# Turning query and index stacks with float32r products instead of pass-through turns

## The reference, cut to what matters

```python
iq = rope_partial(iq.reshape(bsz, t, IDX_HEADS, IDX_DIM), pos)      # 4 heads of 64
ik = rope_partial(ik, pos)
s = jnp.einsum('bthd,bsd->bths', iq, ik_all) * IDX_DIM ** -0.5
score = jnp.einsum('bth,bths->bts', iw, jax.nn.relu(s)) * IDX_HEADS ** -0.5
_, idx = lax.top_k(jnp.where(causal, score, -jnp.inf), topk)         # 256 keys a query
logits = jnp.einsum('btngd,btsnd->btngs', qg, kg) * HEAD_DIM ** -0.5 # 8 query, 2 key heads of 64
p = jax.nn.softmax(jnp.where(valid, logits, -jnp.inf), axis=-1)
o = jnp.einsum('btngs,btsnd->btngd', p, vg)
```

## Time and profile before

| | us |
|---|---|
| median of 3 runs | 1306.44 (1304.9 to 1308.1) |
| the profiled execution's own time | 1305.35 |
| its span | 1303.6 |
| PE busy | 1263.4 (97%) |
| DVE / POOL / ACT busy | 857.0 / 733.3 / 670.5 |

### The profile page before, as it was taken

The page is one execution under the profiler, slowest core; times in us unless marked ns, Lnnn a source line. Parts: engine busy times, 40 slices in busy tenths (PEclk is TensorE's granted clock), DMA queues, the critical chain, the costliest instruction groups (busy, mean ns, idle before and its releaser), DMA issues.

```text
span 1303.6 us, 25268 instructions
## 1 busy us (share of the span) xinstructions
PE 1263.4 (97%) x9537; PEld 1159.3 (89%) x9537; DVE 857.0 (66%) x1586; ACT 670.5 (51%) x1151; POOL 733.3 (56%) x473
## 2 busy tenths in 40 slices
PE   6899999999899999999999999999999999999998
PEld 4677999877766766999999999999999999999998
DVE  5777889889678848677973454555545553644595
ACT  5557988967777776455342343433334336211115
POOL 0242457990152103456587787887878857765620
PEclk8899999999899999999999999999999999999999
DMA  9722106542101127655322243523534268999633
GB/s 347 281 70 74 50 6 213 173 143 82 46 21 30 46 74 228 191 158 146 106 98 66 99 167 133 186 101 130 185 134 170 78 248 311 328 334 347 242 129 131
DMA packets 127274, 198.86 MB, mean 153 GB/s; under 512 B 16839, under 2 KB 100111, under 8 KB 116656
## 3 DMA queue, kind: packets, MB, share of 16 engines
q1 hardware_dynamic: 127008, 193.01, 43.0%
q10 hardware_dynamic: 144, 4.23, 0.8%
HBM read 144.07 MB, written 53.18 MB: 151 GB/s over the span
## 4 chain that ended last, share of the span: by engine, by line
PE 70%; DVE 8%; ACT 5%; POOLq 5%; POOL 3%; DVEq 2%; issue 2%; SPq 2%; ACTq 1%; DMA 1%
PE ps L3508 30%; PE ps L3528 15%; PE ps L3192 2%; PE ps L3206 2%; PE ps L3372 2%; ACT junk L1354 2%; PE ps L3374 2%; PE ps L3373 2%; PE ps L3181 1%; POOLq L1076 1%; DMA ada_shift<-in_ada_w 1%; DVE junk L2073 1%; PE ps L3182 1%; DVEq L2623 1%; PE ps L3325 1%
## 5 line engine op out<-in xcount | busy, mean ns | idle before, releaser
L3528 PE MATMUL ps<-input,down_H 128*128 128x258 f32 x1120 | 180.7, 283 | 1.5 <-DVE acc L2771 1.5
L3528 PEld LDWEIGHTS ps<-input,down_H 128*128 128x128 f32 x1120 | 154.5, 190 | 2.1 <-issue 1.1
L3508 PE MATMUL ps<-comb,opH 128*128 128x258 f32 x960 | 154.4, 283 | 0.0
L1170 POOL TENSOR_TENSOR opL<-wsum,opH 128x512 fp32r<-128x512 f32 x80 | 123.7, 1556 | 36.1 <-ACT opH L1690 32.7
L1690 ACT CAST opH<-wsum 128x512 fp32r<-128x512 f32 x80 | 49.6, 621 | 168.0 <-PE ps L3508 109.6
L3508 PEld LDWEIGHTS ps<-comb,opH 128*128 128x128 f32 x960 | 132.7, 190 | 0.0
L3508 PE MATMUL ps<-h2H,opH 128*128 128x258 f32 x640 | 129.0, 283 | 0.3 <-DVE h2L L2628 0.3
L3508 PE MATMUL ps<-h2H,opL 128*128 128x258 f32 x640 | 129.0, 283 | 0.0
L3508 PE MATMUL ps<-h2L,opH 128*128 128x258 f32 x640 | 128.6, 282 | 0.0
L1013 POOL TENSOR_TENSOR wL<-wraw,wH 128x1024 fp32r<-128x1024 f32 x28 | 70.1, 2504 | 86.9 <-ACT wH L1347 86.7
L2771 DVE TENSOR_TENSOR acc<-ps,acc 128x516 f32<-128x516 f32 x112 | 76.6, 694 | 61.7 <-PE ps L3528 61.2
(11 more groups left out here) (528 smaller groups left out, 3532.1 us busy)
## 6 DMA issues: line engine op xcount, KB each, us to landing
down_inputs<-staged SPq DMA_DIRECT2D x35, 1032.0 KB, 4.9
input<-down_inputs SPq DMA_DIRECT2D x35, 1032.0 KB, 7.1
adb<-in_ada_w SPq DMA_DIRECT2D x8, 2048.0 KB, 8.5
wraw<-in_w_out SPq DMA_DIRECT2D x24, 512.0 KB, 4.5
raw<-in_w_gate SPq DMA_DIRECT2D x10, 1024.0 KB, 6.5
raw<-in_w_up SPq DMA_DIRECT2D x10, 1024.0 KB, 5.2
down_block<-in_w_down SPq DMA_DIRECT2D x5, 2048.0 KB, 11.0
x_feature_major<-x0T ACTq DMA_DIRECT2D x1, 4128.0 KB, 15.2
```

What stands on the lines that cost most here:

```text
L1170: pool.tensor_tensor(opL[g % OPS][:], operand(v, p), opH[g % OPS][:].bitcast(F32), ALU.subtract).then_inc(s_wL, 1)
L3508: ins = mm(ps[:, sum_bank(v, p) + h, 0:HC], weight[s][:, k, :], token[:, k, h * HC:(h + 1) * HC], start=begins, stop=ends, skip_group_chec ...
L3528: ins = mm(ps[:, 2 * m + h, 0:HC], weight[:, f, cc], tok[:, f, part, h * HC:(h + 1) * HC], start=(f == 0 and weight is hi and part == 0), ...
```

## The change

Three places turn their stacks by an ordinary float32r product with the identity, `mm(out, piece.bitcast(F32R), identR, start=True, stop=True)`, in place of the pass-through turn: both loops of `index_transposed` and the one of `q_transposed`. The piece is loaded as weights as before, and the identity streams as before. For this the identity must be a tile that a rounding instruction wrote: SP loads it by a transfer of its own into `identity_loaded`, POOL copies it, rounded, into the new tile `identity`, and TensorE waits for two transfers and the copy. `ident`, with which every other turn works, becomes an fp32 view of that same tile. The identity moves to the end of the table of constants, so that the other constants are one contiguous load of 525 columns.

```diff
-        consts = sb("consts", [P, C_ALL])
-        ident = consts[:, C_ID:C_ID + P]
+        consts = sb("consts", [P, C_ID])
+        identR = sb("identity", [P, P], F32R)
+        ident = identR[:].bitcast(F32)
...
+        unrounded = at("identity_loaded", [P, P], Q5 + 30208)
...
-            sp.dma_start(consts[:], a["consts"]).then_inc(s_const, 16)
+            sp.dma_start(unrounded[:], a["consts"][:, C_ID:C_ALL]).then_inc(s_const, 16)
+            sp.dma_start(consts[:], a["consts"][:, 0:C_ID]).then_inc(s_const, 16)
...
         def _(pool):
+            pool.wait_ge(s_const, 16 * 2)
+            pool.tensor_copy(identR[:], unrounded[:]).then_inc(s_const, 1)
             pool.memset(wbd[:], 0.0).then_inc(s_wbd0, 1)
...
-            pe.wait_ge(s_const, 16)
+            pe.wait_ge(s_const, 16 * 2 + 1)
...
                     for h in range(IH):
-                        tr(ps[:, 4, h * P:(h + 1) * P], istk[s][:, h].rearrange("p r d -> p (r d)"), ident)
+                        mm(ps[:, 4, h * P:(h + 1) * P], istk[s][:, h].rearrange("p r d -> p (r d)").bitcast(F32R),
+                           identR[:], start=True, stop=True)
                 for r in range(2):
-                    ins = tr(ps[:, 5, r * P:(r + 1) * P], ikstk[s][:, r].rearrange("p c d -> p (c d)"), ident)
+                    ins = mm(ps[:, 5, r * P:(r + 1) * P], ikstk[s][:, r].rearrange("p c d -> p (c d)").bitcast(F32R),
+                             identR[:], start=True, stop=True)
...
                 for h in range(GRP):
-                    ins = tr(ps[:, 4 + item % 2, h * P:(h + 1) * P],
-                             stk[:, GRP * (n % 2) + h].rearrange("p r d -> p (r d)"), ident)
+                    ins = mm(ps[:, 4 + item % 2, h * P:(h + 1) * P],
+                             stk[:, GRP * (n % 2) + h].rearrange("p r d -> p (r d)").bitcast(F32R), identR[:],
+                             start=True, stop=True)
```

More of the change, by code:

```diff
@@ L46 @@
 FIRST_SEL = TOPK // P
-C_ID, C_CAUS, C_ONE, C_E4, C_E4T, C_M4, C_E8, C_E8T, C_ROPE = 0, 128, 256, 384, 416, 424, 428, 492, 500
+C_CAUS, C_ONE, C_E4, C_E4T, C_M4, C_E8, C_E8T, C_ROPE = 0, 128, 256, 288, 296, 300, 364, 372
 C_SEL = C_ROPE + ALLT * 2 * HALF
-C_ALL = C_SEL + 9
+C_ID = C_SEL + 9
+C_ALL = C_ID + P
 V_LN1, V_LN2, V_CW, V_CB, V_BA, V_BX, V_LAM, V_GL, V_GA, V_ADA = 0, 8, 16, 32, 36, 40, 44, 48, 52, 56
@@ L2518, in _ @@
             dve.drain()
-            V.tensor_scalar(ddg[:], consts[0:64, C_ID:C_ID + 64], dlg[:, 1024:1025], None, ALU.mult)
+            V.tensor_scalar(ddg[:], ident[0:64, 0:64], dlg[:, 1024:1025], None, ALU.mult)
             dve.drain().then_inc(s_dpn, 1)
@@ L3615, in table @@
     c[:, C_ROPE:C_SEL] = rope.transpose(1, 0, 2).reshape(P, -1)
-    c[:, C_SEL:] = (r[:, None] % 32 == np.arange(9)[None, :])
+    c[:, C_SEL:C_ID] = (r[:, None] % 32 == np.arange(9)[None, :])
     return c
```

## The result

The kernel after takes 1308.6 us (median of 22 runs, 1306.43 to 1312.74), the kernel before 1306.98 (22 runs, 1304.52 to 1309.46) on the same chip: ratio 1.0018, interval 1.0011 to 1.0025. That is 1.6 us by the medians, 2.3 by the means, inside the 0.3% that the prediction called no change, but resolved and on the slow side. The forecast was +0.9. In the profiled executions the span grew from 1303.6 to 1306.4 us, 1.2 us more than the medians did; their mean granted clocks were 0.987 and 0.985.

A forecast was written before the change was run, and what follows sets the result against it. TensorE, busy 97% of the span, was taken to bound the kernel. Attention +0.5, index stage +0.1 and start +0.3 made +0.9 us on 1306.44, so 1307.3 us, range 1303.5 to 1310.5.

The forecast's parts named there:

- the +0.3 for the start: Start: the extra identity transfer on SP's queue delays x and the landing of ada_shift by 0.3 us, bounds 0 to 0.4.
- A step of 0.11 us for either kind: All 104 changed pieces on TensorE: a product takes the same 0.11 us step as a turn.
- The rival at the pace of plain fp32: All 104 pieces: narrow products run like plain fp32, 0.24 us in place of 0.11, +13.5 us; chance 0.04.
- the 0.05 that was given as a sign: Query batches behind value products: the time from batch to next product grows by about 0.05 us.
- 0.055 us for a batch on an empty array: Batches starting on an empty array: a product leaves 0.11 us of weight load open, a turn 0.055, so 0.055 more.
- The chain's nine pieces: Attention, 350 to 440 us: nine pieces of query turns on the chain, 9 x 0.055 = 0.5 us.
- Index stage +0.1: Index stage: two batches on the chain, one starting on an empty array (0.05 us); taken as +0.1 us.
- POOL's copy: Start: identity ready by 5.8 us, hidden under TensorE's wait for x, with some 1 us to spare.
- So the clock rose on turns alone: Start, 6.54 to 12.6 us: TensorE ran only turns and reached full clock, so turns count as work for the clock.
- My rival on the clock: Attention: products near 337 to 347 us bring full clock back earlier, giving 1305.7 to 1303.0 us; chance 0.07.
- What I called chance, at 0.05: Half-clock stretches at the start and at 340 fall differently, about 1.7 us either way; chance 0.05 of leaving the 0.3%.

The follow-up runs named there:

- e1: The changed kernel with all 104 pieces turned in pass-through mode again, the loads, POOL's copy and identity tile kept: 1308.23 us, ratio 1.0002 to before.
- the filled pair: f_filled_with_turns, and the changed kernel (products for all pieces) with the same filler turns: 1303.68 and 1303.96 us.
- e2_queries: The changed kernel with the 40 index pieces turned again, so only the 64 query pieces are products: 1309.37 us, ratio 1.0017 to before.
- e3_index: The changed kernel with the 64 query pieces turned again, so only the 40 index pieces are products: 1307.49 us, ratio 1.0003 to before.
- f_filled_with_products: e1 plus float32r products of the identity that nobody reads, at five places where TensorE waits: 1307.12 us, ratio 1.0002 to before.
- h_first_groups: e1 with products only in query batches 0 to 3 (16 pieces): 1308.73 us, ratio 1.0016 to before.
- d1: e1 with one extra turn ahead of every second query batch, no products: 1308.46 us, ratio 1.0007 to before.
- f_filled_with_turns: e1 plus pass-through turns that nobody reads, at five places where TensorE waits: 1303.68 us, ratio 0.9974 to before.
- g_before_filled: The kernel before, without the plumbing, with filler turns only near 313 and 338 to 345 us: 1306.79 us, ratio 0.9988 to before.
- p4_products_fourfold: The changed kernel with each of the 104 products done four times into the same place: 1339.1 us, ratio 1.0244 to before.
- t4_turns_fourfold: e1 with each of the 104 pieces turned four times into the same place: 1332.23 us, ratio 1.0192 to before.

## Why the prediction was right, and what it missed

**The verdict and the range**: no change by the measure given, with 1308.6 in 1303.5 to 1310.5. The likeliest value, 1307.3, was 1.3 us low, of which 0.5 is that the 3 runs of before lay under the later median. As a difference +0.9 was forecast and 1.6 to 2.3 measured, and that it came as near is in part luck: the +0.3 for the start is not borne out, and some +0.8 by the clock stood in the sum at nothing.

**A step of 0.11 us for either kind**: right. One record each, the same latency, weight loads 0.11 us apart. The rival at the pace of plain fp32, +13.5 us, is out. The start of the next product moved by 0.09 (0.41 to 0.50), not by the 0.05 that was given as a sign; 0.04 comes back one step later.

**0.055 us for a batch on an empty array**: right, and the best-founded number of the prediction: seven steps of 0.04 to 0.07 between e1 and after, seven of 0.05 to 0.07 in the filled pair, and none where the array was loaded. The chain's nine pieces gave +0.5; the filled pair shows +0.50 from 352 to 443.

The Trainium skill's "Ensure logical transpose operations use transpose, as opposed to a standard matmul" (Perfetto Trace Analysis, Transposes) is borne out in direction: e2_queries is slower by 0.06% to 0.27%. The runs show why: an open load and the clock, neither of which the page gives.

**Index stage +0.1**: not contradicted; e3_index is +0.2 us by the medians without the outlier (-0.8 to +1.6 by its interval).

**Start +0.3**: neither shown nor excluded. In the first pair of traces x's first turn moved by 0.39 (its transfer was issued at 2.94 against 2.47), and the landing by 0.05, the lower bound's side. But over all traces TensorE's first product with ada_shift starts at 39.09 and 39.45 without the extra transfer and anywhere from 38.7 to 40.4 in the twelve with it, 39.4 in the mean: a spread wider than the term.

**POOL's copy**: hidden as said, ready at 5.50 (5.8 forecast), with 1.4 us to spare.

**The clock**: here the prediction failed, at the step "So the clock rose on turns alone", where I concluded that the kind of instruction couldn't matter. The observation was right, and it settles only that turns count. It says nothing of products, and I took them as equal because they step at the same pace. They are not, in their mean clocks: fourfold pieces 0.9904 against 0.9850, fillers 0.9920 against 0.9878, both with equal steps at equal places. My rival on the clock was drawn with the wrong sign: "products near 337 to 347 bring the clock back" is the reverse of f_filled_with_products. The Trainium skill's full clock that "doesn't engage for transpose-mode" (TensorE: Matmul & The Clock Gate, Part 4: PE-mode transpose) is contradicted for these fp32 turns by the same runs: it is turns that hold the clock up here. What I called chance, at 0.05, was partly cause. Kernels with query products have mean clocks of 0.98441 (after), 0.98450, 0.98456 and 0.98491, those with turned queries 0.98518, 0.98533, 0.98556 (before) and 0.98591. Pooled, with the plumbing in both, 54 runs with query products have 0.9846 and 34 with turned queries 0.9855. After against before, all chips together, is 0.00115 lower, and at 0.7 us for 0.001 that is 0.8 us, an estimate: with the 0.5 of open loads 1.3 us, of 1.6 to 2.3 measured. That the kinds differ is shown; what in a product makes the difference, no run here takes apart, and the theory in my expectations, of how long each kind streams, is untested.

**What stays open**: e1_plumbing against before (clock 0.98518 and 0.98556) is not resolved, so a few tenths may be the plumbing's. That h_first_groups costs as much as all pieces fits a cost that falls due by the clock in the stage from 335 to 355, but its interval (+1.0 to +3.3 us) overlaps everything from half of the change's cost to more than all, and its one trace has most of its delay elsewhere. And one profile of each kernel shows where half clock fell once, not how often it falls there: e1 has the stretch at 410 as after has, with turns alone, and before and d1 don't; d1 has one at 495 in its place. From 60 to 520 us e1, e3, d1 and h show as much half clock as after, 20.5 us, and before 17.1: the difference between the kinds is seen in the averages over runs and in the fourfold traces, not in these.

## What to carry to other kernels

Two instructions that step at the same pace need not be worth the same to TensorE's clock: before calling an exchange free, see how near the kernel stands to a fall of the clock, and multiply each kind fourfold in a run of its own, which here showed the effect on the mean granted clock plainly (0.9904 against 0.9850, 5 runs each). A batch behind instructions that leave no load done ahead pays the open weight load once, here 0.055 us more; that is small, exactly countable and not worth a new wait elsewhere. Where TensorE idles ahead of a stretch at half clock, filler turns that nobody reads can be worth more than they cost: f_filled_with_turns is the fastest kernel of this study, 0.15% to 0.37% under before, and each place has to be tried, since g_before_filled with three of the five gave 0.03% to 0.22%.

## What the runs showed of the hardware that was not expected

- Pass-through turns of fp32 raised TensorE's mean granted clock more than as many float32r products with the same identity: 0.9904 against 0.9850 as repeated pieces, 0.9920 against 0.9878 as fillers, where before has 0.9856.
- TensorE busy for 20.8 of 22.0 us (p4_products_fourfold, 349 to 371) ran 17.1 us of that stretch at 1.2 GHz, whereas t4_turns_fourfold, busy for 19.1 of 22.0, went back to 2.4 GHz after 6.8 us. A busy TensorE in the profile is no sign that the clock will rise.
- A transfer of 64 KB issued ahead of others moved the issue of the first tile of x from 2.47 to 2.94 us. The landing at 39 us moved by no more than it varies between executions (0.05 us in the first pair of traces, a spread from 38.7 to 40.4 over twelve).
- The place of half clock feeds back on waits: without it near 238 us TensorE reached a wait for POOL early, stood for 2.6 to 4.2 us instead of 1.0 to 1.3, and had half clock there (5 of 14 traces, whatever the change).
